# Low-rank queries and keys of the latent attention: two heads' 64 columns side by side in the array, four heads' 32 rotated columns, one rotation product for four heads

## What is computed

```
cq = rmsnorm(q_lora) * g_q          # 768 values for each of 512 tokens
ckv = rmsnorm(kv_lora) * g_kv       # 256 values for each of 768 tokens
q[h] = cq @ w_uq[h]                 # 96 columns: 64 plain ("nope"), 32 to be rotated ("rope")
q[h][rope] = q[h][rope] * cos + rot(q[h][rope]) * sin
k[h] = concat(ckv @ w_uk[h],        # 64 columns
              rotated shared 32)    # the same for all heads
v[h] = ckv @ w_uv[h]
softmax(q[h] k[h]^T * 96**-0.5) v[h]
```

## Time and profile before

| | us |
|---|---|
| median of 3 runs | 2840.19 (2840.01 to 2841.66) |
| the profiled execution | 2841.61 |
| its span, first to last instruction | 2839.8 |
| PE busy | 2783.8 (98%) |
| DVE busy | 1346.5 (47%) |
| POOL busy | 792.8 (28%) |
| ACT busy | 494.8 (17%) |
| mean granted TensorE clock | 0.995 of full speed |

### The profile page before, as it was taken

How to read it: one execution, slowest core, us unless ns; L and a number is a source line. 1 busy time by engine, 2 the same in 40 slices (tenths; PEclk the granted TensorE clock), 3 DMA queues, 4 the chain that set the end, 5 groups by cost and what they waited for, 6 DMA issues and landing times.

```text
span 2839.8 us, 29160 instructions
## 1 busy us (share of the span) xinstructions
PE 2783.8 (98%) x11560; PEld 1992.5 (70%) x11560; DVE 1346.5 (47%) x2482; ACT 494.8 (17%) x1075; POOL 792.8 (28%) x668
## 2 busy tenths in 40 slices
PE   8999999999999999999999999999999999999997
PEld 3655555554886367866888887785568867888873
DVE  7656565568117454325332335315573325544443
ACT  2100000003017153113100002004540001000011
POOL 1233343341213002411344430110024412444420
PEclk9999999999999999999999999999999999999998
DMA  6333333332210101220222221211002222222211
GB/s 248 122 108 128 105 108 125 97 114 87 75 31 1 46 16 45 88 98 30 104 89 89 89 74 47 94 71 60 31 30 89 89 85 80 83 87 90 89 62 57
DMA packets 51751, 231.63 MB, mean 82 GB/s; under 512 B 4256, under 2 KB 10784, under 8 KB 38176
## 3 DMA queue, kind: packets, MB, share of 16 engines
q1 hardware_dynamic: 40960, 181.17, 18.3%
q0 software_dynamic: 9072, 39.85, 4.1%
q10 hardware_dynamic: 1584, 8.75, 0.8%
HBM read 227.66 MB, written 2.10 MB: 81 GB/s over the span
## 4 chain that ended last, share of the span: by engine, by line
PE 60%; DVE 1%; ACT 0%; issue 0%; DVEq 0%; ACTq 0%
PE banks L652 40%; PE banks L588 15%; PE banks L1136 1%; PE banks L1215 1%; PE banks L1152 1%; PE banks L597 1%; PE banks L762 0%; PE banks L1217 0%; PE banks L1209 0%; DVE rstd L1797 0%; PE banks L1223 0%; PE banks L604 0%; DVE normed L1800 0%; PE banks L1194 0%; DVE rstd L1812 0%
## 5 line engine op out<-in xcount | busy, mean ns | idle before, releaser
L652 PE MATMUL banks<-big 128*128 128x256 f32 (+1 forms) x2240 | 572.2, 403 | 0.0
L2550 POOL TENSOR_TENSOR big<-weight_ring 128x512 f32<-128x512 f32 (+2 forms) x117 | 141.0, 1205 | 1380.1 <-PE banks L652 742.8
L652 PEld LDWEIGHTS banks<-big 128*128 128x128 f32 x2240 | 424.9, 190 | 112.8 <-DVE rpb_rows L1916 2.5
L652 PE MATMUL banks<-big,weight_ring 128*128 128x256 f32 (+1 forms) x1504 | 398.2, 409 | 3.3 <-DVE scratch_a L1922 2.6
L652 PEld LDWEIGHTS banks<-big,weight_ring 128*128 128x128 f32 x1504 | 285.3, 190 | 87.8 <-DVE scratch_a L1922 3.8
L652 PE MATMUL banks<-normed,weight_ring 128*128 128x256 f32 (+1 forms) x1312 | 342.6, 404 | 1.7 <-issue 0.9
L588 PE MATMUL banks<-normed,weight_ring 128*128 128x256 f32 (+4 forms) x944 | 312.1, 484 | 1.2 <-ACT normed L1339 0.6
L652 PEld LDWEIGHTS banks<-normed,weight_ring 128*128 128x128 f32 x1312 | 249.1, 190 | 69.2 <-issue 2.2
L588 PEld LDWEIGHTS banks<-normed,weight_ring 128*128 128x128 f32 (+2 forms) x944 | 174.1, 188 | 117.5 <-issue 100.5
L2551 POOL TENSOR_TENSOR big<-weight_ring 128x512 f32<-128x512 f32 (+2 forms) x142 | 211.0, 1486 | 0.0
L652 PE MATMUL banks<-normed,big 128*128 128x256 f32 (+1 forms) x840 | 203.7, 389 | 0.0
(11 more groups left out here) (431 smaller groups left out, 3333.5 us busy)
## 6 DMA issues: line engine op xcount, KB each, us to landing
weight_ring<-weights SPq DMA_DIRECT2D x144, 1024.0 KB, 4.8
rpb_rows<-w_ada POOLq DMA_DIRECT2D x28, 512.0 KB, 3.6
p_embed<-w_ada POOLq DMA_DIRECT2D x28, 512.0 KB, 3.6
weight_ring<-weights SPq DMA_DIRECT2D x16, 768.0 KB, 4.3
weight_ring<-weights SPq DMA_DIRECT2D x14, 512.0 KB, 3.6
weight_ring<-weights SPq DMA_DIRECT2D x8, 640.0 KB, 3.7
big<-w_ada POOLq DMA_DIRECT2D x2, 2048.0 KB, 8.2
residual<-xT ACTq DMA_DIRECT2D x2, 1536.0 KB, 12.2
```

The costliest lines, as they stand in the source:

```text
L652: last = nc.tensor.matmul(z, stationary(p), moving(p), start=opens and p == 0, stop=p == kp - 1, skip_group_check=True)
L2550: T(w[2], a11, a21, ALU.subtract).then_inc(sums_c, 1)
```

## The change

Queries. The 64 plain columns and the 32 rotated columns of each head are made by products of their own. `uq_nope(t)` takes heads 2t and 2t+1: for each of the six blocks one product of 128 by 64 to partitions 0 to 63 and one to partitions 64 to 127 of bank 4 or 5. `uq_rope(r)` takes four heads: for each block four products of 128 by 32, to partitions 0, 32, 64 and 96 of bank 6. The rotation is one product of 128 by 128 for four heads with a block-diagonal matrix `ROT4`, into bank 7. DVE builds `ROT4` (one memset and four small copies) and copies of cosine and sine for four heads on 128 partitions (eight copies of 32 x 512). For each group of four heads DVE does the two multiplications once on 128 x 512 and four additions of 32 x 512.

Keys. Two heads are made together: partitions 0 to 63 and 64 to 127 of the same bank, alternately.

ACT copies per head pair two times 64 x 512 for the queries, per four heads one 128 x 512, and per head pair four copies for the keys. The signals `unit_begun` of the query units 1 and 3 are given together with those of the units that follow. One semaphore in the second block (`asw["exp"]`), for which nothing waited, is gone, and `rot4` is new.

```diff
-            for h in range(NA_HEADS):
-                n = SEQ["uq"] + h // 2
-                if h % 2 == 0:
-                    begin(n)
-                if h >= 2:
-                    pe.wait_ge(gen["qc"], h - 1)
...
+            def uq_nope(t):
+                begin(SEQ["uq"] + t)
+                if t >= 2:
+                    pe.wait_ge(gen["qc"], t)
                 for k in range(QR):
-                    if h == 0:
+                    if t == 0:
                         pe.wait_ge(lora["normed"], k + 1)
-                    last = mm(bank[0:QK_D, 4 + h % 2, :], slot(n, ((h % 2) * QR + k) * QK_D, QK_D), CQ[:, k, :],
-                              k == 0, k == QR - 1, h % 2 == 0 and k == 0)
+                    for e in range(2):
+                        last = mm(bank[64 * e:64 * e + NOPE, 4 + t % 2, :], uq_columns(2 * t + e, k, 0, NOPE), CQ[:, k, :],
+                                  k == 0, k == QR - 1)
+                        if k == 0 and e == 0 and t % 2 == 0:
+                            last.then_inc(unit_begun, 1 if t == 0 else 2)
                 last.then_inc(gen["q"], 1)
...
+            def uq_rope(r):
+                if r == 1:
+                    pe.wait_ge(gen["qc"], 3)
+                for k in range(QR):
+                    for g in range(4):
+                        last = nc.tensor.matmul(bank[ROPE * g:ROPE * (g + 1), 6, :], uq_columns(4 * r + g, k, NOPE, QK_D),
+                                                CQ[:, k, :], start=(k == 0), stop=(k == QR - 1),
+                                                tile_position=(0, ROPE * g))
+                last.then_inc(gen["q"], 1)
+
+            def q_rotated(r):
+                pe.wait_ge(gen["qc"], 3 * r + 3)
+                if r == 0:
+                    pe.wait_ge(gen["rot4"], 1)
+                else:
+                    pe.wait_ge(gen["q_roped"], 1)
+                return nc.tensor.matmul(bank[:, 7, :], ROT4, Q_ROPE[:, r, :], start=True, stop=True)
+
+            uq_nope(0)
+            uq_nope(1)
+            uq_rope(0)
+            uq_nope(2)
+            q_rotated(0).then_inc(gen["rot"], 1)
+            uq_nope(3)
+            uq_rope(1)
...
-            for h in range(NA_HEADS):
-                if h >= 2:
-                    pe.wait_ge(gen["kc"], h - 1)
...
+            for t in range(NA_HEADS // 2):
+                if t >= 2:
+                    pe.wait_ge(gen["kc"], t - 1)
                 for k in range(KVR):
+                    for at, a, b in ((2 * (t % 2), 0, S), (2 * (t % 2) + 1, S, T)):
+                        for e in range(2):
+                            last = mm(bank[64 * e:64 * e + NOPE, at, 0:b - a],
+                                      slot(n, ((2 * t + e) * KVR + k) * NOPE, NOPE), CKV[:, k, a:b], k == 0, k == KVR - 1)
+                            if (t, k, a, e) == (0, 0, 0, 0):
+                                last.then_inc(unit_begun, 2)
                 last.then_inc(gen["k"], 1)
+                if t == 0:
+                    q_rotated(1).then_inc(gen["rot"], 1)
```

On DVE, after the eight copies of L2281:

```diff
-            for h in range(NA_HEADS):
-                dve.wait_ge(gen["rot"], h + 1)
-                mark(V.tensor_tensor(TMP5[0:QK_D, h % 2, :], bank[0:QK_D, 6 + h % 2, :], con("sin", 0, S, QK_D),
-                                     ALU.mult))
-                link(V.tensor_tensor(QM[0:QK_D, h, :], QM[0:QK_D, h, :], con("cos", 0, S, QK_D), ALU.mult))
...
+            link(V.memset(ROT4, 0.0))
+            for g in range(4):
+                at = slice(ROPE * g, ROPE * (g + 1))
+                last = V.tensor_copy(ROT4[at, at], cst[NOPE:QK_D, CONST["rot"] + NOPE:CONST["rot"] + QK_D])
+            last.then_inc(gen["rot4"], 1)
+            for g in range(4):
+                at = slice(ROPE * g, ROPE * (g + 1))
+                V.tensor_copy(COS4[at, :], cst[NOPE:QK_D, CONST["cos"]:CONST["cos"] + S])
+                last = V.tensor_copy(SIN4[at, :], cst[NOPE:QK_D, CONST["sin"]:CONST["sin"] + S])
+            link(last)
+            for r in range(2):
+                dve.wait_ge(gen["rot"], r + 1)
+                mark(V.tensor_tensor(TMP5[:, r, :], bank[:, 7, :], SIN4, ALU.mult))
+                link(V.tensor_tensor(Q_ROPE[:, r, :], Q_ROPE[:, r, :], COS4, ALU.mult))
+                for g in range(4):
+                    at = slice(ROPE * g, ROPE * (g + 1))
+                    last = V.tensor_tensor(QM[NOPE:QK_D, 4 * r + g, :], Q_ROPE[at, r, :], TMP5[at, r, :], ALU.add)
+                last.then_inc(gen["q_roped"], 1)
```

More of the change, by code:

```diff
@@ L296, in build @@
         NA_BIAS = view(p_sb, 0, 2, 512)
+        COS4, SIN4 = big[:, 8192:8704], big[:, 8704:9216]
+        Q_ROPE = view(big, 9216, 2, S)
+        ROT4 = bm_t[:, 0:P]
         def mla_turned(u):
@@ L438, in build @@
         amla = st("att_mla", "s", "max", "exp", "norm", "t", "tc", "pv", "oc")
-        asw = st("att_sw", "s", "biased", "max", "exp", "norm", "t", "tc", "pv", "oc")
+        asw = st("att_sw", "s", "biased", "max", "norm", "t", "tc", "pv", "oc")
         lora = st("lora", "sq", "sq_used", "root", "normed")
-        gen = st("mla_gen", "kr", "kr_roped", "q", "qc", "rot", "q_roped", "k", "kc", "v", "vc")
+        gen = st("mla_gen", "kr", "kr_roped", "q", "qc", "rot4", "rot", "q_roped", "k", "kc", "v", "vc")
         mrg1, mrg2 = stages(2, "merge", "gate", "free")
@@ L969, in _, with uq_columns @@
                              stop=True).then_inc(gen["kr"], 1)
-            for h in range(NA_HEADS):
-                n = SEQ["uq"] + h // 2
-                if h % 2 == 0:
-                    begin(n)
-                if h >= 2:
-                    pe.wait_ge(gen["qc"], h - 1)
+            def uq_columns(h, k, a, b):
+                at = (h % 2 * QR + k) * QK_D
+                return slot(SEQ["uq"] + h // 2, at + a, b - a)
+            def uq_nope(t):
+                begin(SEQ["uq"] + t)
+                if t >= 2:
+                    pe.wait_ge(gen["qc"], t)
@@ L976, in _ @@
                 for k in range(QR):
-                    if h == 0:
+                    if t == 0:
                         pe.wait_ge(lora["normed"], k + 1)
-                    last = mm(bank[0:QK_D, 4 + h % 2, :], slot(n, ((h % 2) * QR + k) * QK_D, QK_D), CQ[:, k, :],
-                              k == 0, k == QR - 1, h % 2 == 0 and k == 0)
-                last.then_inc(gen["q"], 1)
[L982 to L991, removed]
+                    for e in range(2):
[3 more added lines that the diff above has]
+                            last.then_inc(unit_begun, 1 if t == 0 else 2)
@@ L1013, in _ @@
                 last.then_inc(gen["v"], 1)
-            pe.wait_ge(gen["kc"], NA_HEADS)
+            pe.wait_ge(gen["kc"], NA_HEADS // 2)
             pe.wait_ge(gen["vc"], 6)
-            pe.wait_ge(gen["q_roped"], NA_HEADS)
+            pe.wait_ge(gen["q_roped"], 2)
             def mla_scores(u):
@@ L1593, in _ @@
             act.wait_ge(ana["oc"], NA_HEADS // 2)
-            for h in range(NA_HEADS):
[L1595 to L1600, removed]
+            for i in range(6):
+                act.wait_ge(gen["q"], i + 1)
+                if i % 3 == 2:
+                    A(Q_ROPE[:, i // 3, :], bank[:, 6, :], ACT.Copy, scale=QK_D ** -0.5).then_inc(gen["qc"], 1)
+                    continue
+                t = 2 * (i // 3) + i % 3
+                for e in range(2):
+                    last = A(QM[0:NOPE, 2 * t + e, :], bank[64 * e:64 * e + NOPE, 4 + t % 2, :], ACT.Copy,
+                             scale=QK_D ** -0.5)
+                last.then_inc(gen["qc"], 1)
+            for t in range(NA_HEADS // 2):
+                act.wait_ge(gen["k"], t + 1)
+                for e in range(2):
+                    A(KM[0:NOPE, 2 * t + e, 0:S], bank[64 * e:64 * e + NOPE, 2 * (t % 2), :], ACT.Copy)
+                    last = A(KM[0:NOPE, 2 * t + e, S:T], bank[64 * e:64 * e + NOPE, 2 * (t % 2) + 1, 0:CTX], ACT.Copy)
+                last.then_inc(gen["kc"], 1)
             def mla_exp(u, upto):
@@ L1672, in sw_exp @@
                     A(p, p, ACT.Exp, bias=stat_col(u, e), scale=-1.0,
-                      accum_out=stat_col(u, 2 + e)).then_inc(asw["exp"], 1)
+                      accum_out=stat_col(u, 2 + e))
                 A(stat_col(u, 6, 2), stat_col(u, 4, 2), ACT.Exp).then_inc(asw["biased"], 1)
@@ L2284, in _ @@
             last.then_inc(gen["kr_roped"], 1)
-            for h in range(NA_HEADS):
-                dve.wait_ge(gen["rot"], h + 1)
-                mark(V.tensor_tensor(TMP5[0:QK_D, h % 2, :], bank[0:QK_D, 6 + h % 2, :], con("sin", 0, S, QK_D),
-                                     ALU.mult))
-                link(V.tensor_tensor(QM[0:QK_D, h, :], QM[0:QK_D, h, :], con("cos", 0, S, QK_D), ALU.mult))
-                V.tensor_tensor(QM[0:QK_D, h, :], QM[0:QK_D, h, :], TMP5[0:QK_D, h % 2, :],
-                                ALU.add).then_inc(gen["q_roped"], 1)
+            link(V.memset(ROT4, 0.0))
[16 more added lines that the diff above has]
```

(1 more changed line is left out.)

## The result

The changed kernel takes 2816.97 us (median of 4 runs, 2815.06 to 2819.14) against 2840.93 for the kernel before in the same comparison; the ratio is 0.9913, 95% interval 0.9901 to 0.9924. In a second comparison it came out at 0.9916 (0.9901 to 0.9932). Forecast were 2815.4 us, 24.8 less than before; measured are 24.0 less. The profiled execution has a span of 2815.6 us (forecast 2815.0).

What follows compares the result with a forecast made beforehand. PE, busy 98%, bounds the kernel. Its stage shrinks from 69.15 to 42.9 + 1.3 + 0.15 = 44.4 us, 24.8 us earlier, so 2840.2 - 24.8 = 2815.4 us; range 2813.5 to 2826.5.

Steps and rivals of the forecast that it cites:

- PE's stream is the path: Whole kernel: PE is busy 98% of the span, so a microsecond taken from its stream is one of the kernel.
- Pairs overlap fully, at 512 moving columns too: uq_nope and keys: two 64-column products on neighbouring tiles cost as one; a uq_nope pair of heads takes 5.15 us.
- slots: PE's time unit in the stage from first query to first value product: 0.429 us, one record of 512 moving columns.
- last rival: Query, rotation and key stage: nothing overlaps, by the skill's rule; 104.7 us against 68.6, kernel 2877.6 us; chance 0.01.
- Four at once: uq_rope: four 32-column tiles run together, 12 slots per group of four heads, 5.3 us to the next uq_nope.
- the prediction's other estimate: uq_rope, from the skill's table of measured speedups: 30 slots for both groups instead of 24, 2.7 us higher.
- the row that the argument was read from: L1029, alternating 64 columns of two heads: 24 records in 1.46 us, read as twelve fully overlapping pairs.
- two at a time: Rival in uq_rope: 32-column tiles overlap only in twos, 48 slots instead of 24, + 10.3 us, 2825.7; chance 0.14.
- The rival on the slower side: uq_rope: the four 32-column tiles don't overlap at all, 24 slots become 96, + 30.9 us, 2846.3; chance 0.03.
- Changes of the array: Switches of column width between the stage's parts: six at 0.15 and two at 0.20, 1.3 us.
- Slots of rotation and keys: Rotation 4 slots (16 before); keys 16 slots and 16 half slots (32 and 32 before).
- What could come late: Waits on DVE, ACT and the ring around the stage: all stay covered, tightest ACT's key copies with 0.6 us.

Runs made afterwards that it cites:

- keys_only: The kernel before with only the keys changed, two heads' 64 key columns side by side, queries and rotation as before; 2832.68 us, ratio 0.9966.
- full_width: The changed kernel with weights laid out so one 128 by 128 product replaces two or four side by side, queries and keys; 2817.98 us, ratio 0.9913.
- rope_apart: The changed kernel with the six products of each head together in uq_rope, the four heads one after the other; 2838.09 us, ratio 0.9989.
- nope_apart: The changed kernel with all six products of a pair's first head before the second's in uq_nope; 2830.58 us, ratio 0.9961.
- switches: The changed kernel with uq_nope(1) and uq_rope(0), and uq_nope(3) and uq_rope(1), interleaved block by block; 2820.21 us, ratio 0.9926.

## Why the prediction was right, step by step

- *PE's stream is the path.* Right: 24.80 us fewer in the stage, 24.2 in the span, 24.0 in the medians; the rest is the granted clock.
- *Pairs overlap fully, at 512 moving columns too.* Right: the first two pairs take 936.81 - 926.36 = 10.45 us for 24 slots (10.3). The rule of the Trainium skill (page "TensorE: Matmul & The Clock Gate", Part 3, "The mechanism"), that a weight load overlaps matmuls in flight only in another row group, doesn't hold for column tiles here; keys_only, with half the time for the same records, shows it by itself. Nor does it hold between full-width products: in full_width the records of a group, each with a load of 190 ns on the same 128 rows, start 0.429 us apart, and in rope_apart, where a load takes about 0.11 us, one tile's records start just as far apart, so the loads aren't in that distance. So the rule as the prediction read it was a weak ground for its last rival.
- *Four at once.* Right, 5.29 us where 5.3 was forecast, and not the 6.5 us a group (30 slots for both) of the prediction's other estimate. That four would go as two do had no row behind it and was an extrapolation that came true. The argument for it was sound in its fact and short in its cause. I argued that a product for a free tile isn't held up by one before it, and saw no limit. There is one: the queue of four records for each tile. The change lies inside it, with runs of two, in the order of the row that the argument was read from; the prediction didn't know that the order mattered, and that part was luck. Had the change been written head by head, this reasoning would have forecast the same 24.8 us and been wrong by 12 for the pairs (nope_apart) or 21 for the groups (rope_apart). The chance of 0.14 for two at a time was a chance given to the wrong limit.
- *The rival on the slower side* (2846.3): its price was for tiles that don't overlap at all. The nearest that the runs came was rope_apart, 20.7 us back instead of 30.9, with a ratio of 0.9989 (0.9978 to 1.0001) that can't be told from the kernel before. Nothing in the runs shows a kernel slower than before.
- *Changes of the array*, 0.15 each (0.20 at the rotations), bounded from rows at full width and 64 columns only: right, 0.13 to 0.15 between 64 and 32 in switches. With the end of the stage the forecast has 1.3 + 0.15 us for them, and full_width measured 1.35.
- *Slots of rotation and keys*: right, keys_only 10.32 for 10.3.
- *What could come late*: nothing did. `ROT4` had 4.1 us to spare (1.6 at least forecast), ACT's key copies 0.6 as forecast. DVE's second group was slower than I had it: its four additions took 4.75 us, where the first group's took 2.78, and it ended at 969.0; counted from the stage's start that is 42.6 us, against 41.4 for the 966 that I gave as the most. It ran while POOL was building weight sums (first one at 965.03), and the kernel before has the same slowing of L2290 beside POOL (1.64 us at 967.73, where 0.69 is usual, with POOL at work from 965.89); that they disturb each other was not tried. It had 13 us to spare.

## What to carry to other kernels

Products that use half or a quarter of the array's columns cost as much as full ones, and two or four of them next to each other in the program, on different column tiles, cost as one: look in the trace for the distance between starts, not at durations or at the busy share. Write the loop over tiles innermost, or at most two 32-bit products (four records) on one tile before the next tile's turn; and where the weights can be laid out so that one full-width product does it, that saves the changes of the array, 0.15 us each in the trace (1.35 us here, which the medians can't tell), and most of the instructions. Count the slots of an order before you trust it: a tile is never ahead of the program by more than its queue.

## What the runs showed of the hardware that was not expected

- The runs fit a queue of up to four records (two 32-bit products, the running record among them) for each column tile. PE's program is handed out in order and stops at the first full queue, while the tiles run on from theirs: 20 slots for a run of 12 on each of two tiles, 36 on four, 20 for two and two tiles, 14 and 20 for runs of 6, 12 for runs of 2 or 4. By this, records of one tile do start before earlier records of another. Whether the limit counts records, products or their weight loads too, no run tells: every product here is two records with two loads.
- Going from 64 to 32 columns or back costs 0.13 to 0.15 us (switches), about the 0.14 from full width to 64 columns.
- The clock granted between 37 and 60 us, 0.93 or 1.00, moves everything behind it by up to 1.8 us from one execution to another; what decides it stays open. The length of the stage inside a trace is free of it (44.36 us twice).
